# The conv branch of a two-layer decoder trunk: all of its sums turned by the DMA behind the last tap, in two token tiles

## The chip, the core and the metric

The kernel runs on one core of a Trainium2 chip. The metric is the device time of one execution in microseconds (us). TensorE (PE in the rows) multiplies, VectorE (DVE) and ScalarE (ACT) do the elementwise work, GpSimd (POOL) does a few tiny operations and issues some DMAs, and SyncE's queue (SP) issues the weight loads and the DMA transposes. Each engine takes its instructions strictly in the order of the program; semaphores tie the engines together.

## What is computed

Two layers; in each x runs through a SwiGLU FFN, a mixer and a second FFN, on 256 tokens of 1024 features in float32. The mixer has three branches, each with a gate. The change is in the conv branch:

```python
def conv_module(c_in, conv_w, conv_b, ln_g, ln_b, w_conv_out):
    a, b = jnp.split(c_in, 2, axis=-1)
    u = a * jax.nn.sigmoid(b)
    u_pad = jnp.pad(u, ((0, 0), (CONV_WIDTH - 1, 0), (0, 0)))
    y = lax.conv_general_dilated(u_pad, conv_w[:, None, :], window_strides=(1,), padding='VALID',
                                 dimension_numbers=('NWC', 'WIO', 'NWC'),
                                 feature_group_count=D_CONV) + conv_b
    y = jax.nn.silu(layernorm(y, ln_g, ln_b))
    return y @ w_conv_out
...
merged = gates[:, :, 0] * y_ret + gates[:, :, 1] * y_pool + gates[:, :, 2] * y_conv
x = x + merged @ w_out[l]
```

## The kernel before

**Matmuls.** Every float32 product is three matmuls of rounded parts, hi by hi, hi by lo, lo by hi (lines 434 to 436). Tokens lie in two tiles of 128 (t = 0, 1). The weights stream in halves of 128x2048 (1 MB): SP loads a half into one of seven `raw` buffers, ACT rounds it into `w_hi` (line 840, "cast"), DVE subtracts to get `w_lo` (line 1290, "sub"), and TensorE works on it for 24 matmuls. A load waits until the half seven places ahead of it is used, a cast until the half five places ahead is used.

**The conv branch.** The sums are taken with channels on the partitions: four groups of 128 channels, 31 taps each, 124 instructions of 128x256 on DVE (line 1524), scattered as filler between the other DVE work of the mixer. Layer norm wants tokens on the partitions, so the sums y are turned, normalised, and turned back for the product with `w_conv_out`. A turn by DMA takes three steps: ACT splits the words into 16-bit planes, SP issues a transpose, ACT or DVE joins the planes. Before the change the first two channel groups are finished early and turned by DMA in one piece (`split_y_front`, `turn_y_front`, `y_front_out`); the other two are finished last and turned on TensorE (`turn_y_back`, four 128x128 transposes in the middle of the first conv gate product). Then follow `ln_stat_front`, `ln_stat`, `ln_mean`, `ln_eps` (DVE), a power on POOL (line 1905), `ln_shifts` (DVE), `ln_apply` and `split_yn` (ACT), `turn_yn` (SP), `yn_join` (DVE), `conv_silu` and `conv_high` (ACT), `conv_low` (DVE), one after another, twice for the two tiles.

**TensorE around it,** in this order: the product with `w_ret_out` (10.9 us of matmuls), the conv gates in two blocks `M_GATE_CONV` and `M_GATE_CONV + 1` (10.9 us each), the product with `w_conv_out` (`M_CONV`), a TensorE transpose of the first merged piece, and the product with `w_out` in two blocks. `M_CONV` waits for `conv_low` (`conv_lo_ready`). The order on each engine is written out by hand in one `mixer` function per engine; the tap counts given to `conv_taps` in DVE's set where the filler stands. `merge` multiplies a branch by its gate, frees the accumulator bank and adds the result up. In SP's queue the turns stand between the loads, at places given by the number of the half.

The names used below: the turn of y is `turn_y`, the turn back is `turn_yn`; the last w_out half is the second half of block `M_OUT + 1`, whose sub is `sub(2 * M_OUT + 3)` in DVE's mixer.

## Time and profile before

| | us |
|---|---|
| time before, median of 3 (1124.73 to 1125.09) | 1124.8 |
| the profiled execution's own time | 1124.31 |
| its span, first to last instruction | 1122.5 |
| TensorE busy | 1115.9 (99%) |
| DVE busy | 802.8 (72%) |
| ACT busy | 654.6 (58%) |
| POOL busy | 37.7 (3%) |

Between the span and the profiled execution's own time lie 1.8 us. The granted TensorE clock is 0.999 of full over the span. Two 128x512 matmuls follow each other by 0.227 us in a busy stretch, each row showing 0.39 us since they overlap. The mixer of layer 0 runs from about 190 to 370 us; layer 1 repeats it 555.9 us later with the same distances within 0.1 us, so all rows are from layer 0 where nothing else is said. Rows of an engine that follow each other directly overlap by some 0.09 us too; the step from one start to the next is what an instruction costs.

### The profile page before, as it was taken

The numbers are of one execution on the slowest core, as the hardware profiler recorded it, in microseconds if no ns is written. First come the engines' busy times: TensorE is split into PE (matmuls) and PEld (weight loads), VectorE is DVE, ScalarE is ACT, GpSimd is POOL, SyncE is SP. The second block draws the span as 40 slices with busy tenths as digits, with TensorE's granted clock in tenths as the row PEclk, the third lists the DMA queues.
The fourth block names the chain that finished last, engine by engine and source line by source line (L and its number), as shares of the span: only waits on it lengthen the run. The fifth ranks groups of instructions, "written<-read, shape, count | busy, mean of one in ns | idle before, by whom it ended". The sixth has DMA issues, their size and how long they took to land.

```text
span 1122.5 us, 13054 instructions
## 1 busy us (share of the span) xinstructions
PE 1115.9 (99%) x4997; PEld 923.7 (82%) x4997; DVE 802.8 (72%) x992; ACT 654.6 (58%) x750; POOL 37.7 (3%) x67
## 2 busy tenths in 40 slices
PE   9999999999999999999999999999999999999998
PEld 7888888888888888888888888888888888888886
DVE  6856566899999875655476655378999987665553
ACT  6765446664658765554475554376637577656441
POOL 0100000000200000000000000000002001000000
PEclk9999999999999999999999999999999999999999
DMA  9985665773866786666497666467738667866551
GB/s 367 313 277 197 228 236 180 255 215 125 258 223 194 211 284 216 206 204 225 143 309 240 210 201 228 170 218 249 199 122 281 234 197 231 267 215 225 159 187 38
DMA packets 131822, 245.18 MB, mean 218 GB/s; under 512 B 101024, under 2 KB 101408, under 8 KB 107184
## 3 DMA queue, kind: packets, MB, share of 16 engines
q1 hardware_dynamic: 129408, 237.53, 63.7%
q0 software_dynamic: 1648, 6.06, 1.4%
q8 instruction: 39, 0.64, 0.2%
q10 hardware_dynamic: 704, 0.75, 0.2%
q14 instruction: 23, 0.19, 0.1%
HBM read 219.16 MB, written 1.05 MB: 196 GB/s over the span
## 4 chain that ended last, share of the span: by engine, by line
PE 97%; ACT 1%; DMA 1%; DVE 1%; issue 0%; POOL 0%; POOLq 0%; ACTq 0%; DVEq 0%
PE acc L434 31%; PE acc L435 31%; PE acc L436 31%; PE acc L478 1%; PE acc L483 1%; PE acc L487 1%; DMA retT_planes<-ret_planes 1%; PE ret L701 0%; ACT w_hi L840 0%; PE tr L621 0%; ACT v L1089 0%; ACT ret_planes L1081 0%; ACT pin L1072 0%; PE tr L613 0%; PE ret L633 0%
## 5 line engine op out<-in xcount | busy, mean ns | idle before, releaser
L1290 DVE TENSOR_TENSOR w_lo<-raw,w_hi 128x2048 fp32r<-128x2048 f32 (+2 forms) x204 | 445.6, 2213 | 85.4 <-ACT w_hi L840 85.3
L840 ACT CAST w_hi<-raw 128x2048 fp32r<-128x2048 f32 (+2 forms) x204 | 375.4, 1849 | 215.6 <-PE acc L436 202.4
L434 PE MATMUL acc<-w_hi,xT_hi 128*128 128x512 f32 x1152 | 450.6, 391 | 0.0
L436 PE MATMUL acc<-w_hi,xT_lo 128*128 128x512 f32 x1152 | 448.5, 389 | 0.0
L435 PE MATMUL acc<-w_lo,xT_hi 128*128 128x512 f32 x1152 | 448.2, 389 | 0.0
L436 PEld LDWEIGHTS acc<-w_hi,xT_lo 128*128 128x128 f32 x1152 | 216.2, 188 | 45.2
L434 PEld LDWEIGHTS acc<-w_hi,xT_hi 128*128 128x128 f32 x1152 | 216.3, 188 | 44.9 <-DVE gates L1599 0.4
L435 PEld LDWEIGHTS acc<-w_lo,xT_hi 128*128 128x128 f32 x1152 | 216.3, 188 | 44.1
L1373 DVE SCALAR_TENSOR_TENSOR h<-acc,rs,silu_gate 128x256 f32<-128x256 f32 x88 | 42.5, 483 | 152.1 <-ACT silu_gate L907 152.1
L434 PE MATMUL acc<-w_hi,hT_hi 128*128 128x512 f32 x348 | 135.4, 389 | 0.0
L435 PE MATMUL acc<-w_lo,hT_hi 128*128 128x512 f32 x348 | 135.4, 389 | 0.0
L436 PE MATMUL acc<-w_hi,hT_lo 128*128 128x512 f32 x348 | 135.4, 389 | 0.0
L907 ACT ACTIVATE silu_gate<-acc,rs 128x256 f32<-128x256 f32 x88 | 41.7, 473 | 104.6 <-PE acc L436 102.3
L1524 DVE SCALAR_TENSOR_TENSOR y<-uT,par,y 128x256 f32<-128x256 f32 x240 | 98.2, 491 | 0.0
L434 PEld LDWEIGHTS acc<-w_hi,hT_hi 128*128 128x128 f32 x348 | 65.3, 188 | 13.7
L436 PEld LDWEIGHTS acc<-w_hi,hT_lo 128*128 128x128 f32 x348 | 65.3, 188 | 13.6
L435 PEld LDWEIGHTS acc<-w_lo,hT_hi 128*128 128x128 f32 x348 | 65.3, 188 | 13.4
L892 ACT COPY h_planes<-h 128x512 uint16<-128x512 uint16 x88 | 50.4, 620 | 8.9 <-DVE h L1373 8.9
L1356 DVE COPY hT_whole<-hT_planes 128x1024 uint16<-128x1024 uint16 x44 | 33.3, 757 | 8.7 <-DMA hT_planes<-h_planes 8.6
L874 ACT ACTIVATE xT_hi<-hT_whole,par 128x128 fp32r<-128x128 f32 x80 | 25.6, 391 | 14.3 <-DVE hT_whole L1335 14.0
L1344 DVE SCALAR_TENSOR_TENSOR xT_lo<-hT_whole,par,xT_hi 128x128 fp32r<-128x128 f32 x80 | 22.8, 347 | 13.6 <-ACT xT_hi L874 13.5
L1318 DVE SCALAR_TENSOR_TENSOR x<-acc,x 128x512 f32<-128x512 f32 x23 | 15.9, 689 | 21.1 <-PE acc L436 21.1
(150 smaller groups left out, 657.5 us busy)
## 6 DMA issues: line engine op xcount, KB each, us to landing
raw<-in_weights SPq DMA_DIRECT2D x192, 1024.0 KB, 5.2
raw<-in_weights SPq DMA_DIRECT2D x8, 512.0 KB, 3.5
raw<-in_weights SPq DMA_DIRECT2D x12, 256.0 KB, 7.6
bias<-in_gate_bias POOLq DMA_DIRECT2D x6, 512.0 KB, 6.9
first<-in_first SPq DMA_DIRECT2D x7, 384.0 KB, 5.9
x<-in_x SPq DMA_DIRECT2D x2, 512.0 KB, 12.3
scale_row<-in_pool_scale POOLq DMA_DIRECT2D x2, 512.0 KB, 7.1
hT_planes<-h_planes SPq DMA_TRANSPOSE x54, 3.1
```

The source lines that it names most:

```text
L434: nc.tensor.matmul(o, a_hi, b_hi, start=first, stop=False)
L435: nc.tensor.matmul(o, a_hi, b_lo, start=False, stop=False)
L436: return nc.tensor.matmul(o, a_lo, b_hi, start=False, stop=last)
L840: nc.scalar.copy(w_hi[:, hf % HIGHS, 0:n], raw[:, hf % RAWS, 0:n]).then_inc(hi_split, 1)
L874: nc.scalar.activation(xT_hi[:, k, tokens(t)], x_whole[:, i, :], ACT.Copy, scale=gain(l, norm, k)).then_inc(x_hi_ready, 1)
L892: nc.scalar.copy(h_planes[:, :, :, t, :], h[:, t, :].bitcast(U16).rearrange("p (k n a) -> p a k n", k=2, a=2)).then_inc(h_split, 1)
L907: nc.scalar.activation(silu_gate[:, t, :], acc[:, t, IN_BANK[g], 0:256], ACT.Silu, scale=rs[:, t:t + 1]).then_inc(silu_ready, 1)
L1290: nc.vector.tensor_tensor(w_lo[:, hf % RAWS, 0:n], raw[:, hf % RAWS, 0:n], w_hi[:, hf % HIGHS, 0:n].bitcast(F32), ALU.subtract).then_inc(l ...
L1344: a = nc.vector.scalar_tensor_tensor(xT_lo[:, k, tokens(t)], x_whole[:, i, :], gain(l, norm, k), xT_hi[:, k, tokens(t)].bitcast(F32), ALU. ...
L1356: nc.vector.tensor_copy(hT_whole[:].rearrange("p k n -> p (k n)").bitcast(U16) .rearrange("p (m a) -> p a m", a=2), hT_planes[:]).then_inc ...
L1373: nc.vector.scalar_tensor_tensor(h[:, t, :], acc[:, t, IN_BANK[g], 256:512], rs[:, t:t + 1], silu_gate[:, t, :], ALU.mult, ALU.mult).then_ ...
L1524: a = nc.vector.scalar_tensor_tensor(y[:, c, :], u, par[:, l, w:w + 1], y[:, c, :], ALU.mult, ALU.add)
```

## The change

All four channel groups now go on together: tap k of the four groups stands side by side (`k, c = divmod(i, CH)`), so no group is finished early. The early turn of two groups and the TensorE transposes of the other two are gone. Behind the last tap ACT splits all of y for tile 0 and for tile 1, SP turns each tile, and ACT joins each (`y_out`). The nine last taps are moved ahead of three of the four retention merges. The layer norm's statistics take one instruction of 512 columns per tile in place of two of 256, the shift is made by a negation on DVE and a multiplication on POOL (in place of one instruction on DVE), and `ln_apply` takes one instruction in place of two. Gate tanhs, subs and one cast change places. The diff, cut to its core:

```diff
@@ -231,7 +226,7 @@
         ysilu = v
-        y_front = g_silu[:, :, 0:256]
+        y_tokens = g_silu
 
...
@@ -678,7 +670,7 @@
                 in_block(l, M_GATE_CONV, 0)
-                in_block(l, M_GATE_CONV, 1, mid={4: lambda: turn_y_back(l)})
+                in_block(l, M_GATE_CONV, 1)
                 in_block(l, M_GATE_CONV + 1, 0)
...
@@ -749,14 +741,16 @@
 
-            def turn_y_front(l):
-                sp.wait_ge(y_split, (l + 1) * T)
-                sp.dma_start_transpose(yT_planes[:].rearrange("p a (g n) -> p (a g) n", n=P),
-                                       y_planes[:].rearrange("p a k n -> p (a k n)")
-                                       ).then_inc(y_turned, 16)
+            def turn_y(l, t):
+                sp.wait_ge(y_split, l * T + t + 1)
+                sp.wait_ge(ret_whole, l * T + t + 1)
+                sp.dma_start_transpose(retT_planes[:, t].rearrange("p a h n -> p (a h) n"),
+                                       ret_planes[:, t].rearrange("p a h n -> p (a h n)")
+                                       ).then_inc(y_turned[t], 16)
 
...
                 sp.wait_ge(yn_split, l * T + t + 1)
+                sp.wait_ge(y_whole, l * T + t + 1)
                 sp.dma_start_transpose(retT_planes[:, t].rearrange("p a h n -> p (a h) n"),
...
@@ -816,6 +808,8 @@
                         turn_ret(l, t)
+                    if hf % HALVES == 2 * M_RET + RAWS:
+                        turn_y(l, t)
                     if hf % HALVES == 2 * M_GATE_CONV + 1 + RAWS:
...
@@ -1052,32 +1046,28 @@
 
-            def split_y_front(l, t):
-                act.wait_ge(conv_step, l * CH * TAPS + 2 * TAPS)
-                nc.scalar.copy(y_planes[:, :, 2 * t:2 * t + 2, :],
-                               y[:, 0:2, tokens(t)].bitcast(U16)
+            def split_y(l, t):
+                act.wait_ge(conv_step, (l + 1) * CH * TAPS)
+                act.wait_ge(ret_turned[t], 16 * (l + 1))
+                nc.scalar.copy(ret_planes[:, t],
+                               y[:, :, tokens(t)].bitcast(U16)
                                .rearrange("p c (n a) -> p a c n", a=2)).then_inc(y_split, 1)
 
-            def y_front_out(l):
-                act.wait_ge(y_turned, 16 * (l + 1))
+            def y_out(l, t):
+                act.wait_ge(y_turned[t], 16 * (l + 1))
                 act.wait_ge(ret_ready, (l + 1) * T)
-                nc.scalar.copy(y_front.bitcast(U16).rearrange("p t (n a) -> p a t n", a=2),
-                               yT_planes[:].rearrange("p a (t n) -> p a t n", t=T)
-                               ).then_inc(y_front_whole, 1)
+                nc.scalar.copy(y_tokens[:, t, :].bitcast(U16)
+                               .rearrange("p (h n a) -> p a h n", h=CH, a=2), retT_planes[:, t]
+                               ).then_inc(y_whole, 1)
 
             def ln_apply(l, t):
-                name = ("y", l)
                 act.wait_ge(ln_shift_ready, l + 1)
-                for n, src in enumerate((y_front[:, t, :], bank(name)[:, t * 256:t * 256 + 256])):
-                    a = nc.scalar.activation(pin[:, t, n * 256:n * 256 + 256], src, ACT.Identity,
-                                             bias=ln_shift[:, t:t + 1], scale=ln_rstd[:, t:t + 1])
-                a.then_inc(tr_taken[TURN[name] % 2] if t else yn_ready, 1)
+                nc.scalar.activation(pin[:, t, :], y_tokens[:, t, :], ACT.Identity,
+                                     bias=ln_shift[:, t:t + 1], scale=ln_rstd[:, t:t + 1]
+                                     ).then_inc(yn_ready, 1)
 
             def split_yn(l, t):
-                if t:
-                    wait_tr_taken(act, ("y", l))
-                else:
-                    act.wait_ge(yn_ready, l + 1)
+                act.wait_ge(yn_ready, l * T + t + 1)
                 nc.scalar.copy(ret_planes[:, t],
...
@@ -1174,8 +1164,6 @@
                 gate_tanh(l, POOLED, 0, 1)
-                split_y_front(l, 0)
-                split_y_front(l, 1)
                 head_squares(l, 0)
...
@@ -1201,23 +1189,25 @@
                 gate_tanh(l, RET, 1, 1)
-                y_front_out(l)
                 cast(ahead(M_RET) + 1)
...
                 cast(ahead(M_GATE_CONV))
+                for t in range(T):
+                    split_y(l, t)
+                for t in range(T):
+                    y_out(l, t)
                 cast(ahead(M_GATE_CONV) + 1)
-                cast(ahead(M_GATE_CONV + 1))
                 ln_apply(l, 0)
...
                 split_yn(l, 1)
-                gate_tanh(l, CONV, 0, 0)
-                gate_tanh(l, CONV, 0, 1)
-
+                cast(ahead(M_GATE_CONV + 1))
                 conv_silu(l, 0)
                 conv_high(l, 0)
+                gate_tanh(l, CONV, 0, 0)
                 conv_silu(l, 1)
                 conv_high(l, 1)
+                gate_tanh(l, CONV, 0, 1)
                 gate_tanh(l, CONV, 1, 0)
...
@@ -1508,12 +1498,11 @@
                 for i in range(taps_done[0], min(taps_done[0] + n, CH * TAPS)):
-                    pair, j = divmod(i, 2 * TAPS)
-                    k, c = j // 2, 2 * pair + j % 2
-                    if i < 2:
+                    k, c = divmod(i, CH)
+                    if i >= CH:
+                        dve.wait_ge(conv_step, l * (CH * TAPS) + i - CH + 1)
+                    else:
                         dve.wait_ge(u_whole, l * T + T)
-                    if k:
-                        dve.wait_ge(conv_step, l * (CH * TAPS) + i - 1)
                     w = PAR_CONV_W + c * TAPS + k
...
@@ -1625,21 +1614,13 @@
 
-            def ln_stat_front(l, t):
-                dve.wait_ge(y_front_whole, l + 1)
-                nc.vector.bn_stats(ln_stats[:, t, 0, :], y_front[:, t, :]
-                                   ).then_inc(ln_stats_ready, 1)
-
             def ln_stat(l, t):
-                name = ("y", l)
-                wait_tr_full(dve, name)
-                nc.vector.bn_stats(ln_stats[:, t, 1, :], bank(name)[:, t * 256:t * 256 + 256]
-                                   ).then_inc(ln_stats_ready, 1)
+                dve.wait_ge(y_whole, l * T + t + 1)
+                nc.vector.bn_stats(ln_stats[:, t, :], y_tokens[:, t, :]).then_inc(ln_stats_ready, 1)
 
             def ln_mean(l, t):
-                dve.wait_ge(ln_stats_ready, l * 2 * T + T + t + 1)
-                nc.vector.bn_aggr(ln_mean_var[:, t, :],
-                                  ln_stats[:, t, :, :].rearrange("p a n -> p (a n)")
+                dve.wait_ge(ln_stats_ready, l * T + t + 1)
+                nc.vector.bn_aggr(ln_mean_var[:, t, :], ln_stats[:, t, :]
                                   ).then_inc(ln_mean_ready, 1)
...
@@ -1647,10 +1628,10 @@
 
-            def ln_shifts(l):
-                dve.wait_ge(ln_rstd_ready, l + 1)
-                nc.vector.scalar_tensor_tensor(ln_shift, ln_mean_var[:, :, 0], -1.0, ln_rstd,
-                                               ALU.mult, ALU.mult).then_inc(ln_shift_ready, 1)
+            def ln_negate(l):
+                dve.wait_ge(ln_mean_ready, l * T + T)
+                nc.vector.tensor_scalar(ln_minus, ln_mean_var[:, :, 0], -1.0, None, ALU.mult
+                                        ).then_inc(ln_minus_ready, 1)
 
...
@@ -1745,31 +1726,28 @@
                 gate_z(l, RET, 1, 1)
-                subs(M_RET)
+                sub(l * HALVES + 2 * M_RET + 3)
                 merge(l, RET, 0, 0, merged_ret)
+                conv_taps(l, CH * TAPS)
+                merge(l, RET, 1, 0, merged_ret)
+                sub(l * HALVES + 2 * M_RET + 4)
                 merge(l, RET, 0, 1, merged_ret)
-                conv_taps(l, 5)
-
-                merge(l, RET, 1, 0, merged_ret)
                 merge(l, RET, 1, 1, merged_ret)
-                conv_taps(l, CH * TAPS)
-                sub(l * HALVES + 2 * M_GATE_CONV + 3)
-                for t in range(T):
-                    ln_stat_front(l, t)
                 for t in range(T):
...
                 ln_eps(l)
+                ln_negate(l)
+
+                sub(l * HALVES + 2 * M_GATE_CONV + 3)
                 gate_z(l, CONV, 0, 0)
-                ln_shifts(l)
-
                 gate_z(l, CONV, 0, 1)
                 sub(l * HALVES + 2 * M_GATE_CONV + 4)
+                yn_join(l, 0)
                 sub(l * HALVES + 2 * (M_GATE_CONV + 1) + 3)
-                yn_join(l, 0)
-                gate_z(l, CONV, 1, 0)
                 yn_join(l, 1)
                 conv_low(l, 0)
+                gate_z(l, CONV, 1, 0)
                 sub(l * HALVES + 2 * (M_GATE_CONV + 1) + 4)
...
@@ -1904,6 +1882,10 @@
                                         ALU.pow).then_inc(ln_rstd_ready, 1)
+                pool.wait_ge(ln_minus_ready, l + 1)
+                pool.wait_ge(ln_rstd_ready, l + 1)
+                nc.gpsimd.tensor_tensor(ln_shift, ln_minus, ln_rstd, ALU.mult
+                                        ).then_inc(ln_shift_ready, 1)
 
```

**DVE at the last taps, before.** `y` are the taps, `gates<-gates,acc` with `qk<-qk,gates` is one merge, `w_lo` a sub.

```order
L1290 TENSOR_TENSOR w_lo<-raw,w_hi 128x2048 [waits hi_split] x2
L1599 SCALAR_TENSOR_TENSOR gates<-gates,acc 128x512 [waits gate_ready,mm_done]
L1607 TENSOR_TENSOR qk<-qk,gates 128x512 [waits acc_taken01]
L1599 SCALAR_TENSOR_TENSOR gates<-gates,acc 128x512 [waits gate_ready,mm_done]
L1607 TENSOR_TENSOR qk<-qk,gates 128x512 [waits acc_taken00]
L1524 SCALAR_TENSOR_TENSOR y<-uT,par,y 128x256 [waits conv_step] x5
L1599 SCALAR_TENSOR_TENSOR gates<-gates,acc 128x512 [waits gate_ready,mm_done]
```

The same place now:

```order
L1280 TENSOR_TENSOR w_lo<-raw,w_hi 128x2048 [waits hi_split]
L1588 SCALAR_TENSOR_TENSOR gates<-gates,acc 128x512 [waits gate_ready,mm_done]
L1596 TENSOR_TENSOR qk<-qk,gates 128x512 [waits acc_taken01]
L1513 SCALAR_TENSOR_TENSOR y<-uT,par,y 128x256 [waits conv_step] x9
L1588 SCALAR_TENSOR_TENSOR gates<-gates,acc 128x512 [waits gate_ready,mm_done]
L1596 TENSOR_TENSOR qk<-qk,gates 128x512 [waits acc_taken11]
L1280 TENSOR_TENSOR w_lo<-raw,w_hi 128x2048 [waits hi_split]
```

One sub and one merge stand ahead of the nine last taps, where two subs and two merges stood ahead of the first five.

**DVE from the statistics to the join of the turned-back tile 0, before.** `gates<-acc,rs,bias` is a gate, `ln_small` the tiny layer norm values.

```order
L1630 BN_STATS ln_stats<-g_silu 128x6 [waits y_front_whole] x2
L1636 BN_STATS ln_stats<-tr 128x6 [waits tr_full]
L1641 BN_AGGR ln_mean_var<-ln_stats 128x2 [waits ln_stats_ready]
L1636 BN_STATS ln_stats<-tr 128x6 [waits tr_full]
L1641 BN_AGGR ln_mean_var<-ln_stats 128x2 [waits ln_stats_ready]
L1647 TENSOR_SCALAR ln_small<-ln_mean_var 128x2 [waits ln_mean_ready]
L1544 SCALAR_TENSOR_TENSOR gates<-acc,rs,bias 128x512 [waits mm_done,bias_landed]
L1652 SCALAR_TENSOR_TENSOR ln_small<-ln_mean_var,ln_small 128x2 [waits ln_rstd_ready]
L1544 SCALAR_TENSOR_TENSOR gates<-acc,rs,bias 128x512 [waits mm_done]
L1290 TENSOR_TENSOR w_lo<-raw,w_hi 128x2048 [waits hi_split] x2
L1658 COPY pin<-retT_planes 128x2x512 [waits yn_turned0]
```

And now:

```order
L1619 BN_STATS ln_stats<-g_silu 128x6 [waits y_whole]
L1623 BN_AGGR ln_mean_var<-ln_stats 128x2 [waits ln_stats_ready]
L1619 BN_STATS ln_stats<-g_silu 128x6 [waits y_whole]
L1623 BN_AGGR ln_mean_var<-ln_stats 128x2 [waits ln_stats_ready]
L1628 TENSOR_SCALAR ln_small<-ln_mean_var 128x2 [waits ln_mean_ready]
L1633 TENSOR_SCALAR ln_small<-ln_mean_var 128x2 [waits ln_mean_ready]
L1280 TENSOR_TENSOR w_lo<-raw,w_hi 128x2048 [waits hi_split]
L1533 SCALAR_TENSOR_TENSOR gates<-acc,rs,bias 128x512 [waits mm_done,bias_landed]
L1533 SCALAR_TENSOR_TENSOR gates<-acc,rs,bias 128x512 [waits mm_done]
L1280 TENSOR_TENSOR w_lo<-raw,w_hi 128x2048 [waits hi_split]
L1639 COPY pin<-retT_planes 128x2x512 [waits yn_turned0]
L1280 TENSOR_TENSOR w_lo<-raw,w_hi 128x2048 [waits hi_split]
```

A sub that stood ahead of the statistics stands directly behind the negation, and one of the two subs ahead of the join (`pin`) has moved behind it.

**ACT in the same stretch, before:** casts, `ln_apply` (`pin`), `split_yn` (`ret_planes<-pin`).

```order
L840 CAST w_hi<-raw 128x2048 [waits front_used,raw_landed0]
L840 CAST w_hi<-raw 128x2048 [waits mm_done,raw_landed1]
L840 CAST w_hi<-raw 128x2048 [waits front_used,raw_landed2]
L840 CAST w_hi<-raw 128x2048 [waits mm_done,raw_landed3]
L1072 ACTIVATE pin<-g_silu,ln_small 128x256 [waits ln_shift_ready]
L1072 ACTIVATE pin<-tr,ln_small 128x256
L1081 COPY ret_planes<-pin 128x1024 [waits yn_ready]
```

And now:

```order
L834 CAST w_hi<-raw 128x2048 [waits front_used,raw_landed0]
L834 CAST w_hi<-raw 128x2048 [waits mm_done,raw_landed1]
L1052 COPY ret_planes<-y 128x1024 [waits ret_turned0,conv_step]
L1052 COPY ret_planes<-y 128x1024 [waits ret_turned1,conv_step]
L1059 COPY g_silu<-retT_planes 128x2x512 [waits ret_ready,y_turned0]
L1059 COPY g_silu<-retT_planes 128x2x512 [waits ret_ready,y_turned1]
L834 CAST w_hi<-raw 128x2048 [waits front_used,raw_landed2]
L1065 ACTIVATE pin<-g_silu,ln_small 128x512 [waits ln_shift_ready]
L1071 COPY ret_planes<-pin 128x1024 [waits yn_ready]
```

The two splits and two joins of y stand between the second and the third cast; the fourth cast follows behind `ln_apply` and `split_yn` of tile 1.

**SP in the changed kernel,** with the turn of y and the turn back between the weight loads:

```order
L784 DMA raw<-in_weights 128x2048 [waits front_used]
L747 DMA_TRANSPOSE retT_planes<-ret_planes 128x8x128 [waits ret_whole,y_split] x2
L784 DMA raw<-in_weights 128x2048 [waits mm_done]
L784 DMA raw<-in_weights 128x2048 [waits front_used]
L784 DMA raw<-in_weights 128x2048 [waits mm_done]
L754 DMA_TRANSPOSE retT_planes<-ret_planes 128x8x128 [waits y_whole,yn_split] x2
L784 DMA raw<-in_weights 128x2048 [waits front_used]
```

Before, no turn stood between these loads ahead of the turn back.

**POOL in the changed kernel,** around the layer norm's power:

```order
L1871 TENSOR_TENSOR head_meansq_eps<-head_meansq,small 128x8 [waits head_meansq_ready]
L1874 TENSOR_TENSOR head_rs<-head_meansq_eps,small 128x8 [waits head_eps_added]
L1845 DMA bias<-in_gate_bias 128x1024 [waits acc_taken11,acc_taken10,acc_taken00,acc_taken01] x2
L1883 TENSOR_TENSOR ln_small<-ln_small,small 128x2 [waits ln_var_ready]
L1887 TENSOR_TENSOR ln_small<-ln_small 128x2 [waits ln_rstd_ready,ln_minus_ready]
L1834 TENSOR_TENSOR meansq_eps<-meansq,small 128x1 [waits meansq_ready]
```

The second `ln_small` row, the shift, is new; before, DVE's last `ln_small` row did it.

## Rows read from the trace of the kernel before

**Rows 1.** Chain that ended last, layer 0: start us, us, what

```profile
334.38 0.44 PE tr L528 x4
...
338.91 0.96 ACT pin L1072 x2
339.89 1.05 ACT ret_planes L1081
340.96 3.06 DMA retT_planes<-ret_planes
344.05 0.76 DVE pin L1658
...
347.17 0.70 DVE sideT_lo L1664
```

**Rows 2.** Timeline of TensorE's matmuls at the start of `M_CONV`: start, us, what

```profile
347.40 0.39 PE L436 MATMUL acc<-w_hi,xT_lo 128*128 128x512 f32 x1
347.92 0.50 PE L434 MATMUL acc<-w_hi,sideT_hi 128*128 128x512 f32 x1
```

**Rows 3.** Timeline of the weight loads at the last w_out half

```profile
366.13 0.19 PEld L434 LDWEIGHTS acc<-w_hi,xT_hi 128*128 128x128 f32 x1 [0.19 <-DVE w_lo L1290]
```

**Rows 4.** Timeline of ACT: casts behind `w_ret_out`

```profile
324.19 3.72 ACT L840 CAST w_hi<-raw 128x2048 fp32r<-128x2048 f32 x2 [2.07 <-PE acc L436]
```

**Rows 5.** Groups of ACT by shape: the join of turned planes

```profile
L1064 ACT COPY g_silu<-yT_planes 128x1024 uint16<-128x1024 uint16 x2 | 2.7, 1349 | 0.0
```

**Rows 6.** Timeline of DVE, 320 to 366 us

```profile
320.10 4.49 DVE L1290 TENSOR_TENSOR w_lo<-raw,w_hi 128x2048 fp32r<-128x2048 f32 x2
...
327.16 2.07 DVE L1524 SCALAR_TENSOR_TENSOR y<-uT,par,y 128x256 f32<-128x256 f32 x5
...
336.24 0.42 DVE L1636 BATCH_NORM_STATS2 ln_stats<-tr 128x6 f32<-128x256 f32 x1
...
337.47 0.17 DVE L1647 TENSOR_SCALAR ln_small<-ln_mean_var 128x2 f32<-128x2 f32 x1
337.55 0.75 DVE L1544 SCALAR_TENSOR_TENSOR gates<-acc,rs,bias 128x512 f32<-128x512 f32 x1
...
356.12 0.69 DVE L1623 SCALAR_TENSOR_TENSOR xT_lo<-tr,xT_hi 128x512 fp32r<-128x512 f32 x1
356.89 0.69 DVE L1599 SCALAR_TENSOR_TENSOR gates<-gates,acc 128x512 f32<-128x512 f32 x1
...
363.80 2.29 DVE L1290 TENSOR_TENSOR w_lo<-raw,w_hi 128x2048 fp32r<-128x2048 f32 x1
```

**Rows 7.** Timelines of POOL at 27, 285 and 337 us

```profile
27.60 1.25 POOL L1856 TENSOR_TENSOR meansq_eps<-meansq,small 128x1 f32<-128x1 f32 x1 [7.04 <-ACT squares L884]
...
285.36 4.80 POOL L1890 TENSOR_TENSOR head_meansq<-head_sumsq,small 128x8 f32<-128x8 f32 x1 [93.63 <-ACT squares L1050]
290.24 0.20 POOL L1893 TENSOR_TENSOR head_meansq_eps<-head_meansq,small 128x8 f32<-128x8 f32 x1
...
337.73 0.72 POOL L1905 TENSOR_TENSOR ln_small<-ln_small,small 128x2 f32<-128x2 f32 x1 [16.42 <-DVE ln_small L1647]
```

**Rows 8.** Timelines of DVE at the first two of those times

```profile
26.51 2.29 DVE L1290 TENSOR_TENSOR w_lo<-raw,w_hi 128x2048 fp32r<-128x2048 f32 x1 [1.29 <-ACT w_hi L840]
...
285.21 4.89 DVE L1524 SCALAR_TENSOR_TENSOR y<-uT,par,y 128x256 f32<-128x256 f32 x12
```

**Rows 9.** Timeline of SP: loads three and four (issues at its start and end)

```profile
333.73 3.54 SPq L790 DMA_DIRECT2D raw<-in_weights  x2
```

**Rows 10.** DMA issues, KB each, us to landing: all loads, then one issued at 206.36

```profile
raw<-in_weights SPq DMA_DIRECT2D x192, 1024.0 KB, 5.2
...
raw<-in_weights SPq DMA_DIRECT2D x1, 1024.0 KB, 6.4
```

**Rows 11.** DMA issues from 287.2 to 288: a load, and a turn 0.37 us behind it

```profile
raw<-in_weights SPq DMA_DIRECT2D x1, 1024.0 KB, 5.4
yT_planes<-y_planes SPq DMA_TRANSPOSE x1, 6.1
```

26 lines of the change are left out of this document (9 added, 17 removed).

## The prediction, made before the changed kernel ran

> **What bounds the kernel now.** The table of busy times says TensorE, 99% of the span. So a change pays only by matmuls that it removes or by gaps that it closes, and it costs as soon as somebody hands TensorE an operand later than now. I read the chain that ended last first. It is TensorE throughout, except for one stretch per layer, in front of `M_CONV`: `ln_apply` at 338.91, `split_yn` at 339.89, the turn back at 340.96, its join at 344.05, `conv_low` at 347.17 [rows 1]. Then I looked for the gaps. A busy TensorE starts a matmul every 0.227 us; in front of `M_CONV` the step is 0.52 [rows 2], so 0.29 us are lost there, and about 0.1 more as the pipeline refills. A second place is a near miss: at the last w_out half the weight load waits 0.19 us for DVE's sub, which began at 363.80 and ended at 366.08; the load starts at 366.13 [rows 3, 6]. It costs TensorE next to nothing today, but there is no slack at all. Both places hang on the same engine: DVE works almost without a gap from the mixer's gates to there.
>
> **What it removes from TensorE.** Four transposes per layer, 0.44 us [rows 1]; 0.88 in two layers. If `conv_low` came early enough, the wait would go too, 0.29 + 0.1 per layer [rows 2]. That is the most it can give: 0.85 per layer, 1.7 in all.
>
> **The new chain, from the last tap to the turn of y.** All times are of layer 0. Two casts start at 324.19 and take 3.72 [rows 4]; the two splits stand behind them, and with the overlap of 0.1 between rows the first split starts at 327.8. The taps are done by then: the last retention gate ends its step at 320.10, one sub costs 2.2, one merge 1.33 (two of them fill the stretch from 324.5, where the two subs end, to 327.16), nine taps cost 0.40 each [rows 6, 8], sum 327.2. So moving the taps ahead of the merges just takes DVE out of the way, with 0.5 to spare. The merge behind them frees its bank at 327.9, TensorE asks for it at 330.7; cover 2.8. A split costs 1.05 [rows 1], so the turn of tile 0 goes out at 328.9 and lands 3.06 later [rows 1], at 331.9; tile 1 goes out 1.3 behind it and lands at 333.2. Two joins of 1.35 [rows 5] end at 334.6.
>
> **Statistics and shift.** A statistics instruction of 256 columns takes 0.42 [rows 6]; 512 columns I take at 0.68, estimated by the step of the longer DVE rows (1.05 ns per column). With the aggregate (about 0.25 with its handover, from the distance of 1.23 us from 336.24 to 337.47, which holds two statistics and two aggregates [rows 6]) `ln_eps` starts at 335.6; now it is 337.47. On this reckoning the change is 1.9 us ahead here. The sub now directly behind the negation ends at 338.0; TensorE wants its result at 338.9. Cover 0.9.
>
> **Where the lead goes: POOL beside the sub.** The power takes 0.72 today, and DVE does a gate from PSUM meanwhile [rows 6, 7]. In the changed order DVE begins a sub, a 2.2 us instruction with both inputs in SBUF, about 0.1 before POOL's power starts. The trace shows twice what POOL does then. An addition of one column starts at 27.60 beside a sub that runs until 28.80; it takes 1.25 and ends at 28.85. A multiplication of 128x8 starts at 285.36 beside twelve taps that run until 290.10 and ends at 290.16, 4.80 us, where the next one, beside a gate, takes 0.20 [rows 7, 8]. So I let the power wait for the sub's end: 338.0 + 0.7 = 338.7. The new multiplication takes 0.2 (the nearest row is 0.20) if it finds DVE in the two gates that run to 339.3; it ends at 338.9. Both ends of this cost: 0, if POOL is served at once (shift at 336.9), and 2.2 if the multiplication also meets a sub. I take the blocked power and the free multiplication, because these are the rows with the same kind of neighbour.
>
> The Trainium skill, "SBUF — State Buffer", section "SBUF: two separate sides", says that a DVE instruction with two SBUF inputs and a GpSimd one exclude each other for the whole instruction, and that the one that starts first gets the ports. The two rows agree with the first half. By the second half everything would hang on who starts first; were it POOL, the power would end at 336.6, and only the multiplication would wait, for about 338.2.
>
> **From the shift to TensorE.** `ln_apply` is one instruction of 512 columns, between half and all of the 0.96 of today's two [rows 1]; I take 0.8. From 338.95: `ln_apply` to 339.8, split 1.05, the turn back out at 340.85, against 340.96 now. So the lead of 1.9 is used up. It lands at 343.9, unless loads are ahead of it in SP's queue, the second new cost. A turn behind a load lands after it: issued 0.37 behind a load that took 5.4, it took 6.1, so it landed 1.1 behind it [rows 11]. SP now issues the turns of y, at 328.9 and 330.2, ahead of load two, which goes out at 331.4 in place of 325.5; loads three and four go out at 333.7 and at 336.5 (336.9 less 0.44) [rows 9]. Three megabytes in five microseconds queue up. Load four lands at 341.7 by the median of all loads, at 342.9 by the row of the fourth load of a train spaced 2.7 [rows 10]; with 1.1 more, the turn back could not land ahead of 342.8 to 344.0. That is just covered by 343.9; it has no price of its own, but it takes the worth out of an earlier shift.
>
> Behind the landing DVE now has join, sub, join, `conv_low`: 0.66 + 2.2 + 0.66 = 3.5 from landing to the start of `conv_low`, at 347.45. Before it was 3.1, by way of ACT (344.05 to 347.17 [rows 1]), because both subs were done ahead of the join. ACT is ready at 347.0, so DVE's order decides. From there `M_CONV` starts 0.75 later, as now, at 348.2: 0.3 later than now, although TensorE could have been there at 347.2.
>
> **The price is paid at the last w_out half.** From `conv_low` (347.17) to the end of the last sub (366.08) DVE takes 18.91 [rows 1, 6]. The gate that stood ahead of `conv_low` now stands behind it, +0.66; of that the gap of 0.16 ahead of the merge at 356.89 (it could have started at 356.12 + 0.61 [rows 6]) takes up 0.16. So the last sub ends at 347.45 + 19.41 = 366.86, and TensorE's weight load at 366.91 in place of 366.13 [rows 3]: 0.78 us later than now, per layer, with the transposes' 0.44 already counted, since it waits. Nothing behind it has a gap in which to catch up. Sum: 2 x 0.78 = 1.6. On the profiled execution 1124.31 + 1.6 = 1125.9; the median stands 0.5 above it, so **1126.4 us**.
>
> **Hidden edits.** The removed early splits, early turn and early join lie beside a busy TensorE, and DVE, the pacing engine there, loses nothing by them. Tap order costs nothing: the same 124 instructions, and the wait of a tap is for one four places ahead, long done at 0.40 each. The PSUM bank `tr` used once less per layer: nobody waits for it.
>
> **Rivals.**
> 1. *POOL isn't held, or only its multiplication.* Then the shift is there at 336.9 to 338.2, the turn back goes out at 338.9 to 340.1, and load four decides: landing at 342.8 to 344.0, middle 343.4, `conv_low` at 346.95, last sub at 366.36, 0.3 per layer: 1125.3. For it: the power could be ahead of the sub by a hair. Chance 0.2.
> 2. *The chain is on time.* Also load four lands at 341.2 (4.7 after its issue), the turn back at 342.3, `conv_low` at 345.9; both places are met, and the full 1.7 is gained: 1123.1. For it only the shortest loads. Chance 0.07.
> 3. *Slower: the turns queue behind loads.* If loads two to four bunch up worse, or a turn of y takes as long as the 6.1 of [rows 11], the landing of the turn back slips. It decides from 343.9 on, and each microsecond of slip costs one per layer. With a slip of 1: 1128.4. Chance 0.17.
> 4. *Slower: POOL's multiplication misses the two gates* and waits for the next sub, from 339.3 to 341.5. Then `conv_low` is 2.7 later: 1131.8. It decides if the power ends 0.5 later than I reckon. Chance 0.06.
>
> The forecast keeps 0.5.
>
> **How the numbers follow.** The forecast's own spread is half a microsecond per layer: 1125.5 to 1127.2. Under 1123.1 there is no mechanism, and the on-time case and part of rival 1 lie down to there, so the low end is 1123.4. Upwards I take in the queueing of rival 3 up to 1128.8 and leave out rival 4. About 0.2%, 2.2 us, is what a measurement of this kernel can tell from no change: bounds 1122.6 and 1127.0. Faster than that is out of reach of every case but an unseen one, 0.03. Slower are rivals 3 and 4 and the upper edge of the forecast, 0.17 + 0.06 + 0.06, less a slice of rival 3: 0.27. Same: 0.70.
>
> **What would show it.** POOL's power behind the statistics takes 2.8 us (2.1 of them beside the sub) if I am right, 0.7 if rival 1 is. The first turn of y is issued near 328.9, `ln_eps` starts near 335.6, the turn back is issued near 340.9 and lands near 343.9. `conv_low` starts near 347.4, `M_CONV` near 348.2. The last w_out half waits about 0.5 us for its sub, a new row in TensorE's idle time with DVE's `w_lo` as its releaser. A turn that takes over 3.5 us, or a POOL multiplication over 1 us, would be rival 3 or 4. If TensorE's gap in front of `M_CONV` is gone, rival 2 has won.

## The result, and the profile after

| | us |
|---|---|
| changed kernel, median of 6 runs (1128.14 to 1130.34) | 1128.63 |
| kernel before beside it, median of 6 (1124.72 to 1125.33) | 1124.87 |
| ratio, 95% interval | 1.0033, 1.0023 to 1.0043 |
| profiled execution of the changed kernel, own time / span | 1128.82 / 1127.0 |

The change costs 3.8 us. The prediction said 1.6 (1126.4, range 1123.4 to 1128.8). So the sign is right, the size is less than half of what came, and the time lies just inside the range; it is also past the 0.2% that I had given 27%.

TensorE's table of waits (engine, line, waited for: total us, times, longest) was short in the kernel before: the start-up row alone. Now these two stand ahead of it:

```profile
PE acc L430 <- DVE sideT_lo L1645: 3.4, 2, 2.2
PE acc L430 <- DVE w_lo L1280: 0.8, 3, 0.4
```

`sideT_lo` is `conv_low`: once per layer in front of `M_CONV`, and the longest of the two is 2.2, so the layers are not alike. `w_lo` is a sub, three times: the last w_out half of each layer, and one place that the prediction did not have.

**Where the time goes.** I laid the two traces' matmuls side by side. The changed one is 0.52 us later from the tenth matmul on: loads at the start landed a little later in that execution. Other kernels of this study, with the same start, show 0.0 to 0.8, so this is not the change; I take it off below and call the rest "in the frame of before".

| piece | TensorE later by, at its end | of that new |
|---|---|---|
| start | 0.52 | |
| layer 0: transposes gone, `M_CONV`, last w_out half | 1.50 | 0.98 (-0.49, +1.01, +0.46) |
| layer 1: the same three places | 3.48 | 1.98 (-0.55, +2.06, +0.47) |
| layer 1, seam to the second FFN | 4.14 | 0.66 |
| end of the last matmul | 4.17 | |

0.98 + 1.98 + 0.66 = 3.6; the medians differ by 3.8.

**Layer 0 went as reckoned.** ACT's timeline (start, us, what; in brackets the idle time ahead and who ended it): casts, the two splits of y, their joins, `ln_apply`.

```profile
324.74 3.72 ACT L834 CAST w_hi<-raw 128x2048 fp32r<-128x2048 f32 x2 [3.19 <-PE acc L432]
328.37 1.99 ACT L1052 COPY ret_planes<-y 128x1024 uint16<-128x1024 uint16 x2
332.63 2.59 ACT L1059 COPY g_silu<-retT_planes 128x1024 uint16<-128x1024 uint16 x2 [2.27 <-DMA retT_planes<-ret_planes]
...
339.57 0.82 ACT L1065 ACTIVATE pin<-g_silu,ln_small 128x512 f32<-128x512 f32 x1 [2.59 <-POOL ln_small L1887]
```

POOL's timeline, the power (L1883) and the new multiplication (L1887); it answers to the 0.72 of [rows 7]:

```profile
336.45 2.76 POOL L1883 TENSOR_TENSOR ln_small<-ln_small,small 128x2 f32<-128x2 f32 x1 [14.45 <-DVE ln_small L1628]
339.35 0.19 POOL L1887 TENSOR_TENSOR ln_small<-ln_small 128x2 f32<-128x2 f32 x1
```

DVE's timeline from the second statistics on, to lay beside [rows 1, 6]:

```profile
335.25 0.69 DVE L1619 BATCH_NORM_STATS2 ln_stats<-g_silu 128x6 f32<-128x512 f32 x1 [0.28 <-ACT g_silu L1059]
...
336.19 0.17 DVE L1628 TENSOR_SCALAR ln_small<-ln_mean_var 128x2 f32<-128x2 f32 x1
...
336.34 2.28 DVE L1280 TENSOR_TENSOR w_lo<-raw,w_hi 128x2048 fp32r<-128x2048 f32 x1
...
344.77 0.76 DVE L1639 COPY pin<-retT_planes 128x1024 uint16<-128x1024 uint16 x1 [2.62 <-DMA retT_planes<-ret_planes]
345.42 2.27 DVE L1280 TENSOR_TENSOR w_lo<-raw,w_hi 128x2048 fp32r<-128x2048 f32 x1
347.61 0.73 DVE L1639 COPY pin<-retT_planes 128x1024 uint16<-128x1024 uint16 x1
348.23 0.68 DVE L1645 TENSOR_TENSOR sideT_lo<-v,sideT_hi 128x512 fp32r<-128x512 f32 x1
```

POOL's power starts 0.11 behind the sub of 336.34 and ends 0.6 behind it: 2.76 us in place of 0.72. The multiplication beside the gates takes 0.19. Then join, sub, join, `conv_low`, just as the code says.

TensorE's timeline at the three kinds of place (the normal step is 0.227): the start of `M_CONV` and the last w_out half in layer 0 [rows 2, 3], `M_CONV` in layer 1, and the seam.

```profile
347.38 0.39 PE L432 MATMUL acc<-w_hi,xT_lo 128*128 128x512 f32 x1
348.96 0.50 PE L430 MATMUL acc<-w_hi,sideT_hi 128*128 128x512 f32 x1 [1.20 <-DVE sideT_lo L1645]
...
367.04 0.39 PE L432 MATMUL acc<-w_hi,xT_lo 128*128 128x512 f32 x1
367.64 0.50 PE L430 MATMUL acc<-w_hi,xT_hi 128*128 128x512 f32 x1 [0.21 <-DVE w_lo L1280]
...
904.19 0.39 PE L432 MATMUL acc<-w_hi,xT_lo 128*128 128x512 f32 x1
906.80 0.50 PE L430 MATMUL acc<-w_hi,sideT_hi 128*128 128x512 f32 x1 [2.23 <-DVE sideT_lo L1645]
...
948.51 0.39 PE L432 MATMUL acc<-w_hi,xT_lo 128*128 128x512 f32 x1
949.30 0.50 PE L430 MATMUL acc<-w_hi,xT_hi 128*128 128x512 f32 x1 [0.41 <-DVE w_lo L1280]
```

**Layer 1 did not.** There the turn back of tile 0 was issued at 898.34 and took 4.2 us, where layer 0's took 3.2; load four, ahead of it in the queue, was issued at 893.73 and took 7.2 (6.8 in layer 0). At the seam the turn of x took 3.7, where it took 3.0 before. The views of DMA issues, each over the one or two microseconds in which the turn is issued (last number: us to landing); layer 1's turn back (from 898 to 900) and seam turn (942 to 944):

```profile
retT_planes<-ret_planes SPq DMA_TRANSPOSE x1, 4.2
...
hT_planes<-h_planes SPq DMA_TRANSPOSE x1, 3.7
```

**A third turn at the seam.** The seam's work also began late. Ahead of it stands `turn_merged`, which turns the last merged piece for the product with `w_out`. It was issued at 923.46 and took 4.1, where it took 3.4 before (issued at 919.98). It landed 0.9 behind the load ahead of it in both kernels; that load took 6.6 in place of 5.9. The join that waits for this turn, before and after, each with its idle time:

```profile
923.39 0.76 DVE L1614 COPY pin<-retT_planes 128x1024 uint16<-128x1024 uint16 x1 [0.78 <-DMA retT_planes<-ret_planes]
```

```profile
927.54 0.75 DVE L1603 COPY pin<-retT_planes 128x1024 uint16<-128x1024 uint16 x1 [1.45 <-DMA retT_planes<-ret_planes]
```

So the seam's turn of x went out 0.7 nearer to the matmul that needs it (5.9 us ahead of it, 6.6 before), and took 0.7 longer besides. Before, it landed 3.6 ahead of that matmul, now 2.2 ahead of its place. Over the runs below TensorE waits when it lands less than 2.8 ahead (e10: 2.9 and no gap; e12: 2.5 and a gap of 0.27). By these numbers the cover of 0.8 takes up either delay alone, but not both.

### The profile page after: what moved, and what is told of

Read it like the earlier page. It is cut to its first block, busy times and chain, and to the rows that moved or that the text cites. A ratio compares the mean times of both kernels' runs of the same rounds, so it can differ in the third digit from the quotient of the medians.

```text
span 1127.0 us, 13050 instructions
## 1 busy us (share of the span) xinstructions
PE 1115.9 (99%) x4989; PEld 922.6 (82%) x4989; DVE 801.7 (71%) x988; ACT 658.0 (58%) x748; POOL 42.9 (4%) x69
## 4 chain that ended last, share of the span: by engine, by line
PE 88%; DVE 4%; DMA 3%; ACT 2%; issue 2%; POOL 1%; SPq 0%; POOLq 0%; ACTq 0%; DVEq 0%
PE acc L430 29%; PE acc L432 28%; PE acc L431 28%; DMA retT_planes<-ret_planes 2%; DVE w_lo L1280 1%; DMA hT_planes<-h_planes 1%; PE acc L474 1%; PE acc L479 1%; PE acc L483 1%; ACT w_hi L834 0%; POOL ln_small L1883 0%; DMA first<-in_first 0%; DVE gates L1588 0%; ACT ret_planes L1052 0%; PE tr L613 0%
## 5 line engine op out<-in xcount | busy, mean ns | idle before, releaser
L430 PE MATMUL acc<-w_hi,sideT_hi 128*128 128x512 f32 (+1 forms) x80 | 29.8, 373 | 3.4 <-DVE sideT_lo L1645 3.4
```

The lines of the kernel that those rows point to most:

```text
L430: nc.tensor.matmul(o, a_hi, b_hi, start=first, stop=False)
```

## The experiments

Twelve kernels ran; "median" is beside 1124.8 to 1124.9 for the kernel before in every case. Two questions had to be told apart: which of the new steps holds the chain (POOL, the order on DVE, or the queue of loads), and what lengthens two turns in layer 1 by 0.7 us. The gaps below are what TensorE's step has over 0.227; the step behind a gap is some 0.1 longer too. The interval of each ratio is about 1 us wide to either side, so two kernels of this list that differ by less are told apart by their traces, not by their medians.

**e1: POOL taken out of the chain.** The shift is made on DVE, as before the change, and the sub stands behind it.

```diff
                 ln_eps(l)
-                ln_negate(l)
-
-                sub(l * HALVES + 2 * M_GATE_CONV + 3)
                 gate_z(l, CONV, 0, 0)
+                ln_shifts(l)
+                sub(l * HALVES + 2 * M_GATE_CONV + 3)
                 gate_z(l, CONV, 0, 1)
```

> The changed kernel, with the shift made on DVE again and a gate ahead of the sub, so that POOL's power has no sub beside it. Theory A (POOL's power is held by the sub, 2.76 us in place of 0.72, but behind it the turn back queues behind load four anyway): the power takes 0.72, the turn back is issued 2 us earlier (339.4 in the frame of the changed kernel's trace), but lands only 1 us behind load four, that is 0.3 us earlier than now in layer 0 and about 1 us earlier in layer 1; total 1127.0 to 1128.2. Theory B (the held power is the whole cause): the turn back lands 2 us earlier too, total near 1124.5. Theory C (load four is the whole cause and POOL costs nothing): 1128.6, no difference. The sub now ends about when TensorE needs it, so up to 0.2 us per layer may be lost at the second conv gate block.

Measured: 1129.14 (1127.98 to 1129.15 and one of 1130.31), ratio 1.0037 (1.0025 to 1.0050). Missed: no gain at all, and the +0.5 is inside the intervals. The profiled execution is the slowest of the five; 1.6 us of it is a fall of the clock, which e9 shows again. The power itself came as expected:

```profile
336.74 0.72 POOL L1882 TENSOR_TENSOR ln_small<-ln_small,small 128x2 f32<-128x2 f32 x1 [14.47 <-DVE ln_small L1628]
```

The turn back went out 1.9 us earlier (339.61), took 5.3, and landed at 344.93, where it had landed at 344.75 (this execution starts 0.3 later); in layer 1 it took 6.5. Load four landed at 343.84, 1.1 ahead of it. So its landing hangs on load four. The prediction had said just this of an earlier shift; what it had not said is that the sub, now behind the shift, comes late for the second gate block: new gaps of 0.2 at 339.9 and in layer 1, which cost 0.3 each with the step behind them.

**e2: the order on DVE.** Both subs ahead of the first join, a gate between the joins.

```diff
+                sub(l * HALVES + 2 * (M_GATE_CONV + 1) + 3)
                 yn_join(l, 0)
-                sub(l * HALVES + 2 * (M_GATE_CONV + 1) + 3)
+                gate_z(l, CONV, 1, 0)
                 yn_join(l, 1)
                 conv_low(l, 0)
-                gate_z(l, CONV, 1, 0)
```

> The changed kernel with DVE's order around the joins as before the change: both subs ahead of the first join, the gate between the joins. DVE stood idle for 2.6 us (layer 0) and 3.6 us (layer 1) ahead of the first join, so the sub moves into a hole. Theory A: from the landing of the turn back to conv_low 3.15 us in place of 3.5, and from conv_low to the last sub 18.9 in place of 19.4, 0.85 us per layer, total near 1126.9. If the landing alone decides and DVE's order does not: no difference, 1128.6.

Measured: 1127.01 (11 runs), ratio 1.0024 (1.0016 to 1.0033): 1.6 less than the change. Hit. The losses of 0.46 at both last w_out halves are gone; the gap at the seam (0.60) and those in front of `M_CONV` (1.38 and 1.78) stay, the latter since `conv_low` gets its input no earlier:

```profile
344.62 0.75 DVE L1639 COPY pin<-retT_planes 128x1024 uint16<-128x1024 uint16 x1 [0.70 <-DMA retT_planes<-ret_planes]
...
347.75 0.69 DVE L1645 TENSOR_TENSOR sideT_lo<-v,sideT_hi 128x512 fp32r<-128x512 f32 x1 [0.97 <-ACT sideT_hi L1087]
```

**e3: the turns back ahead of load four** in SP's queue.

```diff
+                if hf % HALVES == 2 * M_GATE_CONV + 1 + RAWS:
+                    for t in range(T):
+                        turn_yn(hf // HALVES, t)
                 if hf >= RAWS:
                     wait_half_used(sp, hf - RAWS)
```

> The changed kernel with one edit in SP's queue: the two turns back are issued ahead of load four, which waits behind them. POOL stays held. Theory A: the turn back is issued at the same time as now, lands 3.05 us later and no more, so 0.2 us earlier than now in layer 0 and 1.2 us earlier in layer 1; total near 1127.2, and the spread of the runs (2.2 us now) shrinks. If the queueing of the turn behind load four is no cause: 1128.6. If the late load four starves a cast instead (it is cast 10 us later): above 1129.

Measured: 1127.99 (7 runs), ratio 1.0029 (1.0018 to 1.0040): 0.6 less, 0.8 short of what I expected, and inside the intervals. In layer 0 the turn took 3.03. In layer 1 it took 3.76, with no load ahead of it that was still under way (the last one landed as the turn went out). That is the first sign that something other than loads holds this turn; the seam gap (0.63) was there too.

**e4: all three together,** with the shift on DVE, and the sub ahead of the last retention merge.

> All three edits on the changed kernel: shift on DVE, a gate beside the power, the sub of the second conv gate block ahead of the last retention merge, both subs ahead of the join, and the turns back ahead of load four. Theory A: the turn back is issued near 339.4 and lands near 342.5 in the frame of the changed kernel's trace, conv_low is done before TensorE asks for it, both gaps close, and only the gain of the removed transposes and waits is left: 1.7 us under the kernel before, near 1123.2. If one of the three is no cause it still gives this; if a further cause exists (the turns of y themselves, contention) it stays above 1124.8.

Measured: 1125.10 (11 runs), ratio 1.0002 (0.9993 to 1.0011), 1.9 above my figure. The turn back landed at 343.06, but two subs in a row kept DVE from it until 344.37:

```profile
339.97 4.49 DVE L1281 TENSOR_TENSOR w_lo<-raw,w_hi 128x2048 fp32r<-128x2048 f32 x2
344.37 0.75 DVE L1640 COPY pin<-retT_planes 128x1024 uint16<-128x1024 uint16 x1
```

The order of e2, right for a late landing, is wrong for an early one. Gaps of 0.40 at both `M_CONV`, and 0.57 at the seam.

**e5: a place in the queue?** The slow turns were always number 74 and number 81 of the queue (counted from 0), in e1 to e4 too. The kernel before has two turns fewer. So I gave it one spare turn per layer, behind its early turn of y, and made DVE's retention work wait for it so that its buffer is free.

```diff
+                sp.dma_start_transpose(spare[:].rearrange("p a (g n) -> p (a g) n", n=P),
+                                       y_planes[:].rearrange("p a k n -> p (a k n)")
+                                       ).then_inc(spare_turned, 16)
...
                 dve.wait_ge(head_rs_ready, l + 1)
+                dve.wait_ge(spare_turned, 16 * (l + 1))
```

> The kernel before, with one spare DMA transpose more per layer, issued right behind the early turn of y into memory that is free then; nobody needs its result, the output is the reference's. In every kernel with the changed turns so far the turn back of tile 0 in layer 1 and one turn of x at the following seam land 0.67 to 0.72 us later than their neighbours, whatever stands in the queue; in the kernel before neither does. Theory D (it is the place in the row of the queue's transfers, which one more turn per layer shifts): here these same two turns take 3.7 to 3.8 us in place of 3.05, conv_low of layer 1 comes 0.7 later and the seam waits about 0.3 to 0.6: total 1125.4 to 1126.1. Theory E (it is something of the changed kernels' own): both turns take 3.05 as before and the total is 1124.8.

Measured: 1129.12, ratio 1.0037 (1.0025 to 1.0050). Missed on both sides, and a badly built probe: the spare turn, behind a load, took 8 us, and DVE waited for it, so the whole filler behind slid:

```profile
297.37 2.16 DVE L1586 SCALAR_TENSOR_TENSOR ua<-ret,head_rs,g_silu 128x128 f32<-128x128 f32 x8 [1.65 <-DMA spare<-y_planes]
```

TensorE lost 1.69 and 2.13 us at the start of the conv gates. What it did tell: turns 74 and 81 took 3.04 and 3.23 here (with packets of code 0.2 and 2.4 us behind their issue), and another (layer 0's seam, number 32) took 4.6, with a packet of code at 386.2 in it, as I saw later. The place in the queue is not the cause.

**e6: POOL free and the turns first,** with the joins in the change's order.

```diff
                 merge(l, RET, 0, 1, merged_ret)
-                merge(l, RET, 1, 1, merged_ret)
+                sub(l * HALVES + 2 * M_GATE_CONV + 3)
...
                 ln_eps(l)
-                ln_negate(l)
-
-                sub(l * HALVES + 2 * M_GATE_CONV + 3)
                 gate_z(l, CONV, 0, 0)
+                ln_shifts(l)
                 gate_z(l, CONV, 0, 1)
+                merge(l, RET, 1, 1, merged_ret)
```

> The changed kernel with the shift on DVE, a gate beside the power, the sub of the second conv gate block ahead of the last retention merge, and the turns back ahead of load four; DVE's order around the joins stays as in the changed kernel. Theory A (held power and queueing hide each other, so freeing POOL alone gained nothing and freeing the queue alone 0.6): together they give what neither gave, the turn back lands at 343.1 in place of 344.75 in layer 0, the total is near 1126.2. If the two simply add up (-0.6 and +0.5): 1128.5. If the joins' order is what is left, e4 at 1125.1 is 1 us faster than this.

Measured: 1124.75 (11 runs), ratio 0.9998 (0.9989 to 1.0007): 3.9 less than the change, better than either figure. e1 alone gave +0.5, e3 alone -0.6. The reading is that each lifts one of two limits that stand at nearly the same time, the shift and load four, so only both together pay. But e6 is not just the sum of e1 and e3: it also places the sub, and a merge, where the sub does not come late. By e1's trace the late sub costs 0.3 per layer, so by estimate some 3.3 of the 3.9 belong to the two limits; a kernel with just the two was not run. DVE's timeline: the shift (L1634) is there 1.8 us sooner, and the join finds its turn at 342.80.

```profile
337.62 0.16 DVE L1634 SCALAR_TENSOR_TENSOR ln_small<-ln_mean_var,ln_small 128x2 f32<-128x2 f32 x1 [0.17 <-POOL ln_small L1883]
...
339.68 2.29 DVE L1281 TENSOR_TENSOR w_lo<-raw,w_hi 128x2048 fp32r<-128x2048 f32 x1
342.80 0.77 DVE L1640 COPY pin<-retT_planes 128x1024 uint16<-128x1024 uint16 x1 [0.83 <-DMA retT_planes<-ret_planes]
```

Left over are 0.17 at layer 1's `M_CONV`, 0.35 at its last w_out half, and 0.49 at the seam; the two slow turns took 3.8 and 3.7.

**e7: e4 with one gate in the time before the landing.**

```diff
                 sub(l * HALVES + 2 * M_GATE_CONV + 4)
+                gate_z(l, CONV, 0, 1)
                 yn_join(l, 0)
                 sub(l * HALVES + 2 * (M_GATE_CONV + 1) + 3)
                 yn_join(l, 1)
```

> All three edits, as in the run before, with one more: the second conv gate and one sub are moved so that DVE is free when the turn back of tile 0 lands (it landed at 343.06 and was joined at 344.37). Theory A: M_CONV's gap of 0.40 us in layer 0 closes and that of layer 1 shrinks to 0.1 or so; total 1124.3 to 1124.6. If the last w_out half then waits for its sub instead, because the gate stands behind conv_low again: 1125.0 as before.

Measured: 1124.96 (11 runs), ratio 1.0000 (0.9991 to 1.0009), 0.4 above the upper figure and near that of the other case (1125.0). Layer 0 has no gap any more; layer 1 has 0.62, 0.38 and 0.65 behind the same two slow turns.

**e8: the kernel before, with the useful half of the change.** Turned partly on TensorE as before; the taps early, TensorE's transposes moved into the first conv gate product, the turns back ahead of load four. One sub, one merge and one cast also move behind the shift and `split_yn`, which the lines below leave out.

```diff
-                in_block(l, M_GATE_CONV, 0)
-                in_block(l, M_GATE_CONV, 1, mid={4: lambda: turn_y_back(l)})
+                in_block(l, M_GATE_CONV, 0, mid={5: lambda: turn_y_back(l)})
+                in_block(l, M_GATE_CONV, 1)
...
                 merge(l, RET, 0, 0, merged_ret)
-                merge(l, RET, 0, 1, merged_ret)
-                conv_taps(l, 5)
-
+                conv_taps(l, CH * TAPS)
                 merge(l, RET, 1, 0, merged_ret)
```

> The kernel before (TensorE turns two channel groups) with what the change moved kept and what it added left out: the nine taps ahead of three merges, the TensorE transposes in the first conv gate product of tile 0 instead of tile 1, the sub of the second gate block and a merge behind the shift, the turns back ahead of load four. Theory A: the conv chain is then 3 us ahead, both of TensorE's gaps close, the 0.44 us of transposes per layer stay: 1124.8 - 0.8 = 1124.0. If the gap in front of M_CONV stays, the chain is not what it hung on: 1124.8.

Measured: 1124.18 (11 runs), ratio 0.9995 (0.9986 to 1.0004). Near its figure, but no difference that can be told. The gap in front of `M_CONV` is gone in both layers, and a new one of 0.51 stands at layer 0's seam. There a turn of x took 4.6, and a packet of code lay in it. The view of DMA traffic from 383.2 to 383.5 (queue, kind: packets, MB, share), and the issues from 382 to 383:

```profile
q8 instruction: 1, 0.02, 34.7%
...
hT_planes<-h_planes SPq DMA_TRANSPOSE x1, 4.6
```

That row is what had been missing: **the engines' code comes over the same DMA engines.** In every kernel from e1 to e7 in which turns 74 and 81 were slow, such a packet lies in each. A packet in the flight is not enough, though: in e5 one lay in each of the two, and in e8 the turn back of layer 1 took 3.11 with one 2.44 behind its issue. In the changed kernel there is one packet from 901.1 to 901.3, in the flight of the turn back (898.34 to 902.58), and one at 944.3, in that of the seam turn (942.58 to 946.30):

```profile
q14 instruction: 1, 0.01, 12.0%
```

By counting in the trace: the 16 KB packets of q8 come with about every 126th matmul (110 to 147 between two). The 8 KB packets of q14 belong to the other engines; at those of 166.3, 294.6, 406.2, 515.8 and 631.6 ScalarE had begun 193, 321, 450, 576 and 703 instructions, 126 to 129 apart (in layer 1 the distances are less even, 120 ahead of the packet of 901.2). So an edit that changes how many instructions an engine has moves all later packets of that engine, and decides which turn one falls into. e9 to e12 test that, by instructions that do nothing: waits for something long there, where the engine idles anyway.

```diff
                 gate_tanh(l, RET, 1, 1)
+                for _ in range(12 if l else 0):
+                    act.wait_ge(par_landed, 16)
...
                 x_join(l, norm, 0, 0)
+                for _ in range(16 if (l, norm) == (1, 3) else 0):
+                    dve.wait_ge(par_landed, 16)
                 x_low(l, norm, 0, 0)
```

Two such waits make one instruction, so this is six and eight.

**e9: the changed kernel, code moved.**

> The changed kernel with six instructions more on ScalarE (in front of the cast for the second half of w_ret_out) and eight more on VectorE (in the seam to the second FFN), in layer 1 alone; each is a wait for something long there, put where the engine idles 3.2 and 1.35 us. In the trace of the changed kernel two turns took longer than the 3.04 of their neighbours, and in each a packet of the kind `instruction` fell, 8 KB on q14: at 901.2 in the turn back (898.34, took 4.24) and at 944.3 in the turn of x at the seam (942.58, took 3.72). By the counts of instructions the first comes with every 128th instruction of ScalarE, the second with every 128th of VectorE. Theory F, the fetch of code delays the turn that is under way: the packets come at about 893 and 940, where no turn is under way; the turn back is bound by load four alone and lands about 901.9 in place of 902.6, the turn of x takes 3.05; TensorE's gap in front of M_CONV in layer 1 is 1.7 in place of 2.4, that at the seam is gone (0.65). Sum 1.3 less: 1127.3. Theory P, the delay belongs to the place of the turn in the queue: turns and gaps stay as they were, 1128.6.

Measured: 1128.81 (5 runs, 1127.43 to 1129.77), ratio 1.0033 (1.0020 to 1.0045): the time missed theory F's 1127.3. The trace shows one half of it. VectorE's packet came at 940.2, with no turn under way, and the seam turn, issued between 942 and 944, took 3.1:

```profile
hT_planes<-h_planes SPq DMA_TRANSPOSE x1, 3.1
```

The other packet stayed in the turn back (900.6), and this turn took 3.8. `M_CONV`'s gap was 1.95. The seam kept a gap of 0.31, and lost 0.4 in place of 0.66. Behind `M_CONV`'s gap the granted clock of TensorE fell in this execution to the lower of its two levels, which took back more than both gave; the view by stretches (us, busy of each engine, clock, DMA share, GB/s):

```profile
904.00:907.00 3.00, 1.21 (x6) 0.70 (x5) 3.00 (x5) 2.97 (x8) 0.00 (x0) 1.00 0.97 399
907.00:911.00 4.00, 4.00 (x12) 3.13 (x12) 3.42 (x4) 3.97 (x6) 0.00 (x0) 0.57 0.43 180
```

Eight steps there are 0.40 to 0.43 in place of 0.23, 1.6 us lost in all; e1's profile has the same stretch, the changed kernel's has not. It may be why e9's runs spread by 2.3 us.

**e10: e6, code moved** by the same six and eight.

> The kernel of the run e6_pool_and_turn (1124.75) with the same six and eight instructions more. There the turn back of layer 1 took 3.77 and the turn of x at the seam 3.7, with packets of code at 897.1 and 940.1 in them, and TensorE had gaps of 0.17, 0.35 and 0.49 behind them. Theory F: both take 3.05, the first and the last gap are gone, the middle one is 0.2 or less: 0.7 to 0.9 less, 1123.9. Theory P: 1124.75, turns at 3.7.

Measured: 1123.66 (11 runs, 1123.08 to 1124.65), ratio 0.9990 (0.9981 to 0.9999), 1.1 less than e6. VectorE's packet came at 935.3, the seam turn took 3.05, and the seam's gap of 0.49 was gone. ScalarE's packet stayed at 897.0, and the turn back took 3.8.

**e11: the kernel before, made to be hit.** Eight instructions more on VectorE.

> The kernel before with eight instructions more on VectorE at the same seam of layer 1, where it idles 1.35 us. The turn of x there is issued at 938.4 and takes 3.04; VectorE's packet of code comes at 946.1, behind it. With eight more it comes at about 939.6, in this turn. Theory F: the turn takes 3.6 to 3.8, TensorE has a new gap of about 0.6 near 945, and the time is 1125.4. Theory P, or if what hurt was anything else in the changed kernel: the turn takes 3.04, no gap, 1124.85.

Measured: 1124.81 (11 runs), ratio 0.9999 (0.9990 to 1.0008). Inconclusive: no packet fell into the turn. The two packets near it were at 935.2 and 946.1, as before, and only the last one moved (1115.1 to 1107.5). I had taken the one of 946.1 for VectorE's; by the counts it is SyncE's. The run still serves as a control: eight waits more on VectorE, with no packet moved in or out of a turn, change nothing (1124.81).

**e12: e10 with thirty instructions on ScalarE** in place of six.

> The kernel of the run e10 with thirty instructions more on ScalarE in the place of six (waits for something long there, in an idle time of 3.2 us in front of the cast for the second half of w_ret_out, layer 1; they take 0.07 us each there, 2.1 in all). In e10 the packet of code that was meant to move stayed in the turn back of layer 1 (897.0; the turn took 3.79) and behind it lay gaps of 0.22 + 0.11 in front of M_CONV and 0.34 at the last w_out half. Theory F: with thirty the packet comes near 878, where no turn is under way; the turn back, issued 894.6, takes 3.05 and lands 897.7, both gaps are gone or under 0.1, and the time is 1123.66 less 0.5: 1123.1. If the packet stays at 897.0, it isn't tied to ScalarE's count, and the turn takes 3.8 again: 1123.7, and theory F has no further test. Theory P, the delay belongs to this turn's place: the packet is gone from the turn and the turn still takes 3.8, 1123.7.

Measured: 1123.23 (11 runs, 1122.69 to 1123.73), beside 1124.93 (15 runs), ratio 0.9984 (0.9975 to 0.9993). Hit. From 893 to 902 there is no packet of code, and the turn back took 3.05. First e10, then e12, each DVE's join of the turn back in layer 1 and what it waited for:

```profile
898.43 0.76 DVE L1644 COPY pin<-retT_planes 128x1024 uint16<-128x1024 uint16 x1 [1.59 <-DMA retT_planes<-ret_planes]
```

```profile
897.99 0.77 DVE L1644 COPY pin<-retT_planes 128x1024 uint16<-128x1024 uint16 x1 [0.85 <-DMA retT_planes<-ret_planes]
```

In e12 load three also landed earlier, 0.7 behind the issue of the turn in place of 1.6 in e10. That is not what shortened the turn: in layer 0 of e9 a turn back with a load still under way for 1.7 us and no packet took 3.05, and in layer 1 of e3 one with no load under way and a packet took 3.76.

In e12 `M_CONV` starts one normal first step (0.34) behind its neighbour:

```profile
901.88 0.39 PE L432 MATMUL acc<-w_hi,xT_lo 128*128 128x512 f32 x1
902.22 0.50 PE L430 MATMUL acc<-w_hi,sideT_hi 128*128 128x512 f32 x1
```

So the delay leaves with the packet, at both turns, and does not belong to the turn's place. e12 is also clearly faster than the kernel before, and e10 just (its interval ends at 0.9999); no other kernel here is. Its gain is 1.7. What it still loses: 0.34 at layer 1's last w_out half, and a gap of 0.27 at the seam, with a turn of x of 3.05.

**What is left at the seam** in e9 and e12 goes with `turn_merged`. It took 4.4 and 4.3 there, and 3.9 in e10, where the seam has no gap. In all ten kernels made from the change it took 3.9 to 4.4, and a 16 KB packet of TensorE lay 1.1 to 1.6 us behind its issue; in the four made from the kernel before it took 3.2 to 3.5, and the packet had come earlier, in the turn in front, where it cost nothing. This view of the changed kernel is from 924.6 to 924.9:

```profile
q8 instruction: 1, 0.02, 18.3%
```

The change takes eight transposes off TensorE, so this packet too may have been moved by an instruction count. That it is what makes the load and the turn longer is read from the traces; no run moved it alone.

## Why the prediction was right, and where it was wrong

The time lies inside the range, and the direction is right, but that is in part luck: the upper end was set for a queue of loads, and 0.66 us of the 3.8 come from a place that the prediction did not have. In the frame of before (row less 0.55), layer 0:

| step | predicted | measured |
|---|---|---|
| first split of y | 327.8 | 327.8 |
| turns of y issued | 328.9, 330.2 | 328.9, 330.2 |
| they land | 331.9, 333.2 | 332.1, 333.3 |
| `ln_eps` | 335.6 | 335.6 |
| power ends, multiplication ends | 338.7, 338.9 | 338.7, 339.0 |
| turn back out | 340.85 | 340.95 |
| load four lands | 341.7 to 342.9 | 343.2 |
| turn back lands | 343.9 | 344.2 |
| `conv_low` starts | 347.45 | 347.7 |
| `M_CONV` starts | 348.2 | 348.4 |
| last sub ends | 366.86 | 367.0 |
| cost of the layer | 0.78 | 0.98 |

- **POOL beside the sub: right.** 2.76 in place of 0.72 is the 2.8 expected; the multiplication's 0.19 too. Rivals 1 and 4 are out. By the Trainium skill, "SBUF — State Buffer", "SBUF: two separate sides", the one that starts first gets the ports: here the sub was 0.11 ahead, so the trace agrees. In the other order it does not: in the kernel before, POOL's power on 128x8 ran from 290.51 for 1.65 us, a sub began beside it at 291.27, and the sub took its normal 2.29.
- **The order on DVE and the last w_out half: right.** The loss of 0.46 there appeared in both layers, and e2, which undoes just that order, removed it. That is 0.9 of its 1.6 us; most of the rest is the gap at `M_CONV` of layer 1, 1.78 in place of 2.39.
- **"It has no price of its own": wrong.** This was the step on load four. I let it land by 342.9 at most and called the turn just covered. It landed at 343.2 in layer 0 (worth 0.2 to 0.3) and took 7.2 in layer 1. The bound came from a load of 6.4 in a train spaced 2.7 [rows 10]; here two turns of y and three loads go out within 7.5 us, which the prediction had listed itself, and load four took 6.8. Rival 3, the queue, had the mechanism and its deciding point (343.9), and was rated a rival at 0.17.
- **The layers alike: wrong, and the larger part.** Forecasting one layer and doubling it missed that the turn back of layer 1 met load four (landing 900.9) and, on top, a packet of code: 901.9 would be the landing by the load alone (1.0 to 1.1 behind it), it was 902.6. This turn of 4.2 is the sign of "over 3.5" that the prediction had given to rival 3. `M_CONV` of layer 1 lost 2.06 where layer 0 lost 1.01. Taking load four away (e3) gave 0.6; taking the packet away shortened the turn by 0.7 (e12).
- **The seam: not in the prediction.** 0.66, from two delays of 0.7 each, less the cover of 0.8, plus 0.1 behind the gap. One is the turn of x that took 3.7 in place of 3.0. Its cause is a packet of code, which the change's instruction counts moved there: e9 and e10 moved it off and the turn took 3.05. The other is `turn_merged`. With the packet of the turn of x gone, e9 lost 0.4 there and e10 nothing. It had been "nothing behind it has a gap in which to catch up"; the text never asked what would be *newly* late behind it.

So of the 2.2 us that came on top of the forecast (3.8 against 1.6): 0.2 is layer 0's load four; 1.2 layer 1's, of which 0.7 is the packet; 0.66 the seam. That leaves 0.1. The ceiling of the gain, 0.85 per layer, was sound: TensorE is 0.9 ahead at `M_CONV` of layer 0 in e10 and e12.

What stays open: the rule by which a packet is called for. Six instructions more on ScalarE did not move its packet (901.2 to 900.6, 897.1 to 897.0), thirty did. And whether VectorE's packet can be brought into the seam turn of the kernel before: e11 did not manage it. Kernels made from the kernel before are hit all the same: in e5 and e8 a 16 KB packet lay in the turn of x at layer 0's seam, it took 4.6, and TensorE had a gap of 0.46 and 0.51.

## What to carry to other kernels

When a chain is moved ahead, look for the next limit that stands at nearly the same time, here a load ahead of the transpose in the same queue: lifting one gave nothing (e1), the other little (e3), both, with the sub put in its place, 3.9 us (e6). Order the waiting engine's work by when the transfer lands, and redo that order when the landing moves (e4). In a kernel with no slack, a change in the number of instructions moves the packets of code, and with them 0.7 us here and there, so compare two kernels by their gaps and the landings of each transfer before less than a per mille is credited to the edit.

## What the runs showed of the hardware

- A DMA transpose of 128 partitions of 2 KB took 3.0 to 3.2 us when nothing was under way ahead of it, mostly 3.04. The turn back landed 1.0 to 1.1 us behind load four where that load had over 2 us to go at the issue, however early the turn was issued (5.3 us in layer 0 of e1; the 6.5 in its layer 1 is 1.7 behind the load, with a packet of code in it).
- A packet of code in the flight of a transpose, over all fourteen traces, where no load ahead had over 1.75 us to go. With 8 KB (q14): up to 1.1 us behind the issue it did nothing (34 turns, 3.02 to 3.18); 1.7 to 1.8 behind, the turn took 3.5 to 3.7 (9 turns); 2.3 to 2.5 behind, 3.7 to 3.8 in nine turns and 3.05 to 3.26 in sixteen. With 16 KB (q8): 0.6 to 1.3 behind, 3.4 to 4.6 (32 turns); 2.4 to 3.0 behind, 3.0 to 3.1 in eighteen turns and 4.7 to 4.9 in nine near 1060 us. Why one place is hit and another not is open. The Trainium skill, "Runtime: NRT & Kernel Launch", "Instruction fetch mechanics", says that each engine streams its code by DMA in blocks of 16 KiB, with a cost that is mostly hidden. The trace agrees on TensorE's blocks; the other engines' packets are 8 KB here. TensorE itself shows no cost either (in the kernel before, it has 39 such packets and, from 15 us on, no gap over 0.1 but the two in front of `M_CONV`), but the transposes do.
- TensorE's granted clock fell to the lower of its two levels (1.2 in place of 2.4 GHz) behind gaps of 2.2 us (e1) and 1.95 us (e9) in layer 1's `M_CONV`; over the four microseconds from 907 it was 0.58 and 0.57 in the mean, and cost 1.6 us. It stayed at 1.00 behind the gap of 2.4 in the changed kernel. The gap alone does not decide it.
